# Gates and branch outputs projected token-major, merged rows turned ahead of w_o

## What is computed

```python
y_a = short_conv_mixer(a_b, a_c, a_h, conv_w) @ w_br_a        # each (256, 512) @ (512, 1024)
y_b = hgrn2_mixer(...) @ w_br_b
y_c = chunked_sgu(...) @ w_br_c
merged = sigmoid(gate_a) * y_a + sigmoid(gate_b) * y_b + sigmoid(gate_c) * y_c
return merged @ w_o                                           # gate_* are columns of h @ w_in, 1024 each
```

## Time and profile before

| | us |
|---|---|
| runs shown | 1537.89, 1541.11, 1539.92 (median 1539.92) |
| the profiled execution | 1537.35 |
| its span, first to last instruction | 1535.6 |
| granted TensorE clock, mean | 0.996 of full speed |
| layer 0: branch c, from its first gate matmul to that of b | 34.63 |
| layer 0: branch b, to the first of w_o | 34.56 |
| layer 0: w_o | 23.32 |

### The profile page before, as it was taken

How to read it: one execution, slowest core, us unless ns; L and a number is a source line. 1 busy time by engine, 2 the same in 40 slices (tenths; PEclk the granted TensorE clock), 3 DMA queues, 4 the chain that set the end, 5 groups by cost and what they waited for, 6 DMA issues and landing times. The chain is left out here.

```text
span 1535.6 us, 26186 instructions
## 1 busy us (share of the span) xinstructions
PE 1514.2 (99%) x9449; PEld 1366.9 (89%) x9449; DVE 1297.6 (85%) x1492; ACT 958.8 (62%) x1103; POOL 31.8 (2%) x46
## 2 busy tenths in 40 slices
PE   8999999999999999999999999999999999999997
PEld 7999999999999999999988888888888888888886
DVE  7996888787774797878699999999999999999998
ACT  3535444544534534544388788888878888788785
POOL 0000000000000000000010000000000000000100
PEclk9999999999999999999999999999999999999999
DMA  9943789388984643979479999999999999999993
GB/s 348 334 145 125 259 274 315 110 278 283 326 310 133 206 137 110 343 285 369 170 268 395 410 394 408 391 365 408 367 383 390 364 411 363 389 376 376 411 393 145
DMA packets 228897, 471.01 MB, mean 307 GB/s; under 512 B 16156, under 2 KB 130004, under 8 KB 228820
## 3 DMA queue, kind: packets, MB, share of 16 engines
q1 hardware_dynamic: 225056, 457.27, 82.0%
q0 software_dynamic: 3488, 12.59, 2.1%
q10 hardware_dynamic: 276, 0.09, 0.0%
HBM read 454.69 MB, written 15.21 MB: 306 GB/s over the span
## 5 line engine op out<-in xcount | busy, mean ns | idle before, releaser
L1215 ACT ACTIVATE split<-raw 128x1024 fp32r<-128x1024 f32 x750 | 783.8, 1061 | 368.4 <-PE psU L667 172.7
L1947 DVE TENSOR_TENSOR split<-raw,split 128x1024 fp32r<-128x1024 f32 x528 | 617.1, 1220 | 22.7 <-ACT split L1215 10.8
L667 PE MATMUL psU<-split,yS 128*128 128x512 f32 x2112 | 484.9, 390 | 0.2 <-DVE split L1947 0.2
L667 PE MATMUL psU<-hS,split 128*128 128x256 f32 x3840 | 471.9, 284 | 7.4 <-DVE split L1450 4.8
L667 PEld LDWEIGHTS psU<-hS,split 128*128 128x128 f32 x3840 | 465.0, 192 | 10.4 <-issue 7.0
L667 PEld LDWEIGHTS psU<-split,yS 128*128 128x128 f32 x2112 | 395.0, 188 | 82.0 <-DVE split L1947 0.8
L1450 DVE TENSOR_TENSOR split<-raw,split 128x1024 fp32r<-128x1024 f32 x222 | 264.3, 1219 | 63.6 <-ACT split L1215 63.2
L667 PE MATMUL psA<-split,hidE 128*128 128x512 f32 x1056 | 246.0, 392 | 0.0
L667 PEld LDWEIGHTS psA<-split,hidE 128*128 128x128 f32 x1056 | 196.4, 188 | 40.2
L1528 DVE SCALAR_TENSOR_TENSOR adacc<-raw,cact,adacc 128x1024 f32<-128x1024 f32 x56 | 71.8, 1282 | 3.9 <-DVE adacc L1528 0.5
L667 PE MATMUL psU<-yS,split 128*128 128x256 f32 x576 | 70.1, 283 | 0.0
(11 more groups left out here) (256 smaller groups left out, 845.8 us busy)
## 6 DMA issues: line engine op xcount, KB each, us to landing
raw<-in_moe_w_dram SPq DMA_DIRECT2D x496, 512.0 KB, 5.9
raw<-in_w_in_dram SPq DMA_DIRECT2D x116, 512.0 KB, 5.5
raw<-in_ada_w_dram SPq DMA_DIRECT2D x96, 512.0 KB, 7.5
raw<-in_ffn_w_dram SPq DMA_DIRECT2D x66, 512.0 KB, 7.1
raw<-in_moe_w_dram SPq DMA_DIRECT2D x64, 256.0 KB, 6.0
raw<-in_w_o_dram SPq DMA_DIRECT2D x16, 512.0 KB, 8.7
token_rows<-sc SPq DMA_DIRECT2D x11, 512.0 KB, 9.6
raw<-in_w_br_a_dram SPq DMA_DIRECT2D x8, 512.0 KB, 9.8
```

The lines of the kernel that those rows point to most:

```text
L667: return pe.matmul(o, a, b, start=start, stop=stop, skip_group_check=True)
L1215: return act.activation(o, i, ACT.Copy)
L1947: TTN(split[:, slot, 1, :], raw[:, (RAW0 + n) % RAW, :], split[:, slot, 0, :].bitcast(F32), ALU.subtract).then_inc(s_lo, 1)
```

## The change

Gates and branch outputs are made token-major. A branch is now two halves of 512 columns. A half is four gate pieces (256 rows by 512 columns) into two banks, one for each 128 tokens, and then two y pieces into two banks: 12 matmuls of 512 columns per piece. The list of pieces follows: the eight `ada_w` pieces of a section stand behind the eight gate pieces, four in each half. `merged` now has tokens on the partitions, so TensorE turns it in 128x128 blocks into two spare banks of psA: the first half between gates and y of the last half of b, the second half after the first w_o piece. The copies into the halves of `hS` read these banks. The order of the w_o pieces is changed so that three pieces need only the first half. ScalarE copies the branch input into `yS` ahead of the gates, and for that waits until the branch before has used its last y piece. VectorE's `low_parts` and the products of `ada_part` are put in the order of the new list.

```diff
+WO_ORDER = [(0, 0), (1, 0), (0, 1), (1, 1), (2, 0), (2, 1), (3, 0), (3, 1)]
...
-        elif kind in ("i", "v", "ffn"):
-            used += 4 if key[-1] % 2 == 0 else 0
+        elif kind in ("i", "v", "ffn", "gatea", "gateb", "gatec", "ya", "yb", "yc"):
+            used += (2 if kind[0] == "y" else 4) if key[-1] % 2 == 0 else 0
...
-            used += 1 if kind[0] == "y" else 2
+            used += (3, 1, 2, 2)[key[-1]] if kind == "wo" else 2
...
-            gates = [("split", "w_in", l, q * 512, GATE0[b] + 256 * j, 256) for j in range(4) for q in range(2)]
             ada = section() if b != BRANCHES[0] else []
-            for q, gate in enumerate(gates):
-                out += [gate] + ada[q:q + 1]
-            out += [("split", "w_br_" + b, l, 0, 256 * j, 256) for j in range(4)]
-        out += [("split", "w_o", l, q * 512, 256 * j, 256) for j in range(4) for q in range(2)]
+            for hh in range(2):
+                for q in range(4):
+                    out += [("split", "w_in", l, q * 256, GATE0[b] + 512 * hh, 512)] + ada[4 * hh + q:4 * hh + q + 1]
+                out += [("split", "w_br_" + b, l, q * 256, 512 * hh, 512) for q in range(2)]
+        out += [("split", "w_o", l, q * 512, 256 * j, 256) for j, q in WO_ORDER]
...
+            def half_rows(banks, nq, x):
+                for q in range(nq):
+                    w = next_split()
+                    for tt in range(TT):
+                        for kk in range(2):
+                            for wp, hp in ((0, 0), (1, 0), (0, 1)):
+                                last = mm(banks[tt][:, :], x[:, hp, 2 * q + kk, tt * P:(tt + 1) * P],
+                                          w[wp][:, kk * 512:(kk + 1) * 512], (q, kk, wp, hp) == (0, 0, 0, 0),
+                                          (q, kk, hp) == (nq - 1, 1, 1))
+                    last.then_inc(s_used, 1)
+
+            def turn_merged(l, i, bank):
+                pe.wait_ge(s_mg, 8 * l + 4 + 2 * (i // 2) + 2)
+                if i > 1:
+                    pe.wait_ge(s_ml, 4 * l + i - 1)
+                for m in range(2):
+                    col = (2 * i + m) % 4 * P
+                    for tt in range(TT):
+                        row = merged[:, 4 * (i // 2) + 2 * tt:4 * (i // 2) + 2 * tt + 2, :].rearrange("p a b -> p (a b)")
+                        last = pe.transpose(bank[:, m * T + tt * P:m * T + (tt + 1) * P], row[:, col:col + P], ident[:, :])
+                last.then_inc(s_mt, 1)
...
                 for n, b in enumerate(BRANCHES):
...
+                    for hh in range(2):
+                        half_rows([open_unit((l, "gate" + b, 2 * hh + tt)) for tt in range(TT)], 4, hS)
+                        if (n, hh) == (2, 1):
+                            scale, spare0 = open_event(("ada", 6 * l + 4))
+                            stat, spare1 = open_event((l, "norm2"))
+                            turn_merged(l, 0, spare0)
+                            turn_merged(l, 1, spare1)
+                        banks = [open_unit((l, "y" + b, 2 * hh + tt)) for tt in range(TT)]
+                        if hh == 0:
                             pe.wait_ge(s_yl, 3 * l + n + 1)
...
+                        half_rows(banks, 2, yS)
...
+                for j, q in WO_ORDER:
+                    if (j, q) == (1, 0):
+                        turn_merged(l, 2, spare0)
+                        turn_merged(l, 3, spare1)
...
@@ ScalarE @@
                 for n, b in enumerate(BRANCHES):
+                    act.wait_ge(s_y, 3 * l + n + 1)
+                    if n:
+                        act.wait_ge(s_used, SIGNAL[l, "y" + BRANCHES[n - 1], 3][1])
+                    src = {"a": AH, "c": UB, "b": YB}[b]
+                    copy(yS[:, 0, :, :].rearrange("p a b -> p (a b)"), src).then_inc(s_yh, 1)
...
-                        if j == 0:
-                            act.wait_ge(s_y, 3 * l + {"a": 1, "c": 2, "b": 3}[b])
-                            src = {"a": AH, "c": UB, "b": YB}[b]
-                            copy(yS[:, 0, :, :].rearrange("p a b -> p (a b)"), src).then_inc(s_yh, 1)
-                high_parts(SIGNAL[l, "gateb", 3][2] + 4 + 4)
-                for j in range(4):
-                    act.wait_ge(s_mg, 8 * l + 4 + j + 1)
-                    copy(hS[:, 0, 2 * j:2 * j + 2, :].rearrange("p a b -> p (a b)"),
-                         merged[:, 2 * j:2 * j + 2, :].rearrange("p a b -> p (a b)")).then_inc(s_mh, 1)
+                merged_high(0)
+                merged_high(1)
+                high_parts(SIGNAL[l, "yb", 3][2] + 4)
+                merged_high(2)
+                merged_high(3)
...
@@ VectorE @@
-                    gates = SIGNAL[(l, "gate" + BRANCHES[n], 0)][2] - 2
+                    gates = SIGNAL[(l, "gate" + BRANCHES[n], 0)][2] - 4
...
-                low_parts(SIGNAL[l, "gatea", 3][2])
...
                 branch_low(0)
+                low_parts(SIGNAL[l, "gatea", 0][2] + 2)
 
                 for n, b in enumerate(BRANCHES):
                     if n:
-                        ada_part(n, range(4))
+                        ada_part(n, range(2))
                         branch_low(n)
-                        ada_part(n, range(4, KD))
+                        ada_part(n, range(2, KD))
...
-                            if n == 2 and j:
+                            if n == 2 and j % 2:
+                                if j == 1:
+                                    low_parts(SIGNAL[l, "yb", 2][2])
                                 merged_low(j - 1)
-                            if n == 2 and j == 3:
-                                merged_low(3)
+                                merged_low(j)
```

More of the change, by code:

```diff
@@ L111, in unit_plan @@
         for b in BRANCHES:
-            plan += [((l, "gate" + b, j), "A") for j in range(4)]
-            plan += [((l, "y" + b, j), "D") for j in range(4)]
+            for hh in range(2):
+                plan += [((l, "gate" + b, 2 * hh + tt), "A") for tt in range(TT)]
+                plan += [((l, "y" + b, 2 * hh + tt), "D") for tt in range(TT)]
         plan += [((l, "wo", j), "D") for j in range(4)]
@@ L159, in unit_signals @@
             signal[key] = ("used", used, used)
-        elif kind in ("i", "v", "ffn"):
-            used += 4 if key[-1] % 2 == 0 else 0
+        elif kind in ("i", "v", "ffn", "gatea", "gateb", "gatec", "ya", "yb", "yc"):
+            used += (2 if kind[0] == "y" else 4) if key[-1] % 2 == 0 else 0
             signal[key] = ("used", used, used)
-        elif kind in HEAD_GROUPS or kind in ("gatea", "gateb", "gatec", "wo", "ya", "yb", "yc"):
-            used += 1 if kind[0] == "y" else 2
+        elif kind in HEAD_GROUPS or kind == "wo":
+            used += (3, 1, 2, 2)[key[-1]] if kind == "wo" else 2
             signal[key] = ("used", used, used)
@@ L415, in program @@
         s_mg = sem("merged_ready")
+        s_mt = sem("merged_rows_turned")
         s_sel = sem("selection_ready")
@@ L895, in mixer @@
                 for n, b in enumerate(BRANCHES):
-                    for gg in range(2):
-                        for _ in project(lambda j: (l, "gate" + b, 2 * gg + j)):
-                            pass
-                    for j in range(4):
-                        bank = open_unit((l, "y" + b, j))
-                        if j == 0:
-                            pe.wait_ge(s_yl, 3 * l + n + 1)
[L903 to L908, removed]
+                    for hh in range(2):
+                        half_rows([open_unit((l, "gate" + b, 2 * hh + tt)) for tt in range(TT)], 4, hS)
[6 more added lines that the diff above has]
+                        if hh == 0:
+                            pe.wait_ge(s_yl, 3 * l + n + 1)
+                        half_rows(banks, 2, yS)
                     if n == 0:
@@ L914, in chunk_m @@
                         pe.wait_ge(s_ml, 4 * l + k // 2 + 1)
[L915 to L927, removed]
+                wo = {}
+                for j, q in WO_ORDER:
+                    if (j, q) == (1, 0):
+                        turn_merged(l, 2, spare0)
+                        turn_merged(l, 3, spare1)
+                    if q == 0:
+                        wo[j] = open_unit((l, "wo", j))
+                    w = next_split()
+                    for m in range(2):
+                        for kk in range(4):
+                            if j == 0 and m == 0:
+                                chunk_m(4 * q + kk)
+                            last = tile(wo[j][:, m * T:(m + 1) * T], w, 4 * q + kk, kk * 256 + m * P,
+                                        q == 0 and m == 0 and kk == 0, q == 1 and kk == 3)
+                    last.then_inc(s_used, 1)
                 stat_sum(stat, l)
@@ L1314, in mixer, with merged_high @@
                             act.activation(half(OSQ, 1), banks[1][:, :], ACT.Square).then_inc(s_osq, 1)
+                spares = [psA[2 * (EVENT_AT[e] % 2) + 1] for e in (("ada", 6 * l + 4), (l, "norm2"))]
+                def merged_high(i):
```

(14 more changed lines are left out.)

## The result

The changed kernel took 1545.14 us in the median of six executions, the kernel before 1537.92 us in six (the three shown above and three more): a ratio of 1.0047 (95% interval 1.0035 to 1.0058), 7.2 us or 0.47% slower. The forecast was 1543.6 against 1539.92, 3.7 us slower.

A forecast was written before the change was run, and what follows sets the result against it. TensorE, busy 99% of the span, was taken as the bound. Wider matmuls (−11.5 us) and transposes (+3.5) gave −8.0; with waits for operands the sum became +3.7, so 1539.92 + 3.7 = 1543.6 us, range 1533.5 to 1547.5.

The forecast's parts named there:

- The gain: Six branch passes: 144 matmuls of 512 columns replace 288 of 256, saving 1.9 us each, 11.5 in all.
- The turns: Two groups of eight TensorE transposes added per layer, 0.88 us a group, 3.5 us in all.
- Branch a: y starts at 169.8 after 3.5 us idle, pass ends at 191.6: net −0.3 us in each layer.
- The hand-over: At each change of branch TensorE waits for VectorE's low parts: 3.5 us in b, 0.5 in c.
- Into w_o: TensorE waits 1.4 to 1.5 us for merged rows before the second turn group; w_o costs +2.1 us per layer.
- DMAs: Later piece loads cost 0; up to 6 us if layer 1's cover goes, a rival with chance 0.12.
- The sum: Layer 0 +2.8 us and layer 1 +0.95, together +3.7 us.
- The number: Whole kernel: 1539.92 + 3.7 = 1543.6 us, in terms of the median of the runs shown.
- the feeds keep up: Rival: low parts reach b's first y piece before TensorE, holes go, −11 us on the sum, 1532.6; chance 0.2.

The follow-up runs named there:

- run 1: Changed kernel, with ScalarE making the high parts of the next branch's third and fourth gate pieces before waiting for the last y piece: 1532.89 us, ratio 0.9976.
- run 2: Changed kernel, with only the third gate piece's high part made ahead of ScalarE's wait for the last y piece: 1540.43 us, one execution.
- Run 7: The kernel of run 4, with VectorE merging the last two y units of b before the low parts of w_o's third and fourth pieces: 1523.74 us, ratio 0.9916.
- run 4: Changed kernel with both reorderings, that of run 1 and that of run 3: 1526.73 us, ratio 0.9931 to the kernel before.
- run 6: Kernel before, with only VectorE's last normalisation steps moved behind its low parts of branch a: 1533.50 us, ratio 0.9976.
- run 3: Changed kernel, with VectorE's last normalisation steps moved behind the low parts of yS and of branch a's first two y pieces: 1537.62 us, ratio 0.9997.

## Why the prediction was right, and where it was short

The direction and the mechanism held. Step by step:

- *The gain.* 0.2267 us per 512-column matmul against 0.2268; branch c, where no long hole stands, gave −1.5 and −2.0 against −1.5 and −2.05. Neither figure of the Trainium skill (TensorE: Matmul & The Clock Gate, Back-to-back issue gap), the isolated N/2.4 + 2.5 ns and the sustained 131 ns at 512 columns, holds for these matmuls.
- *The turns.* Eight transposes took 261.38 − 260.59 = 0.79 us, 0.88 forecast.
- *Branch a.* The y pieces started at 169.83 against 169.8, though the hole was 2.9 us and not 3.5: the gates began at 155.78, not at 155.4, since 48 matmuls from 149.64 on took 6.14 us and not the 5.76 reckoned. The pass was to end at 191.6. It ended at 193.31: 1.7 us of this are the 24 matmuls at the lower clock. In layer 1, where the clock stayed up, the step was right to 0.2 us.
- *The hand-over.* From the first gate matmul of b to that of y it took 242.54 − 228.17 = 14.4 us, and 14.4 was forecast; start to start that is the forecast hole of 3.5. Runs 1 and 2 show that ScalarE's wait sets it.
- *Into w_o.* A hole of 0.95 measured, 1.5 forecast: the merged rows stood at 270.9, 3.9 us past the end of y and not 4.3. Run 7 shows that the cause was the one named, low parts ahead of the merges.
- *DMAs.* No hole in front of a gate piece in layer 1, and TensorE's only waits there are the three holes; taking 0 was right. The reserve was smaller than written, though: the 5.5 us to landing is the median of the whole kernel, and around c and b of layer 1 the w_in loads took 10.3 in the kernel before and 12.0 in the changed one.
- *The sum.* The term that is missing is the price of a hole beyond its length. The prediction priced holes as idle time only, at 2 × (3.5 + 0.5 + 1.5) and branch a's. The clock added 1.7 in a and 1.7 in b of layer 0 and 1.4 in b of layer 1, 4.8 us. Filling the holes gave back as much within the noise: by the two ratios, 1.0047 − 1.0008 = 0.0039 of 1538, 6.0 us, with some 2.5 us of uncertainty. In other executions the fourth place is slow too (7.18 us for the 24 matmuls in a of layer 1 in run 1, 640.38 to 647.56), so the mean price can be higher than 4.8. In the profiled pair 1.6 of it came back behind w_o of layer 1. With +4.8, the −2.0 there and the −0.4 and −0.3 at w_o the 3.7 becomes 5.8; 0.4 is left for small terms.
- *The number.* The forecast of 1543.6 us lies nearer to the measured 1545.14 than its working deserves, and that part is luck: its base, 1539.92, came from three executions and is 2.0 us above the median of six. The change itself was 7.2 us, twice the 3.7 forecast; as a ratio 1.0024 was forecast, below the interval measured.

The rival "the feeds keep up" gave 1532.6 and would have been a saving of 7.3 on the median shown. It did not happen, but run 1 shows that its condition was one line away. Its price was set too low: the ratios of runs 4 and 7, 0.9931 and 0.9916, are 10.6 and 12.9 us below the kernel before. What it left out is branch a, whose hole the old kernel had as well. As run 6 shows, 3.7 us of run 4's gain belong to that reordering and the other 6.9 to the wide matmuls with their turns, with some 3.5 us of uncertainty. The prediction's account for these is 8.0 without holes; less the two holes of 0.95 at w_o that run 4 still has, it is 6.1.

## What to carry to other kernels

When a change makes an engine's work arrive in larger lots, write down each feeding engine's queue at the seams, in order, from the last event of the old lot: the hole is found by adding starts (14.4 us worked out, 14.4 measured), and it shrinks by what is taken off that queue (1.19 us for one operation of 1.14). Look first for a wait in a copying engine that stands ahead of work which does not depend on it. And price a hole in a TensorE stream above its length: here one of 2 to 3.5 us cost up to 1.7 us more behind it.

## What the runs showed of the hardware

The traces of the changed kernel and of runs 1 to 3 have twelve holes of 2 us and more in the mixer. The 24 matmuls behind ten of them took 6.87 to 7.19 us at a mean granted clock of 0.76 to 0.79: both of 2.13 us, all four of 3.32 or 3.33, and four of the six of 2.88 to 2.90. Behind the other two of 2.90 (643.22 in the changed kernel, 170.84 in run 2) the clock stayed at 1.00. Behind the holes of 1.06 to 1.24 us in the kernel before it stayed at 1.00 too: 96 matmuls of 256 columns took 11.58 or 11.59 us. What decides between falling and staying these runs don't tell.

The clock also fell in the normalisation behind w_o, where the trace shows TensorE busy without a hole: to a mean of 0.69 over 11.0 us in layer 0 of run 1, while the same stretch of the changed kernel ran at 1.00. So one profiled execution can lie well off the median of its kernel, as that one did (1539.67 against 1532.89).

A float32 matmul of 256 columns on plain float32 operands shows as two records, 0.208 us each; the same width in the float32r passes is one of 0.120.
